# Head by head instead of head pairs on TensorE, and a small two-engine exchange moved to another stage, in a two-block fp32 kernel

## The reference, cut to what matters

```python
    cb = jnp.einsum("bclgn,bcsgn->bcgls", cc, bc)
    y_diag = jnp.einsum("bcgjls,bcsgjp->bclgjp", cb[:, :, :, None] * decay_in, x_)
    y_off = jnp.einsum("bclgn,bcgjpn,bcgjl->bclgjp", cc, prev, jnp.exp(a_cum))
    return (y_diag + y_off).reshape(b, s, h, p)
```

```python
    lb = jax.nn.softmax(lower_bounds.astype(jnp.float32), axis=0)
    lb = jnp.cumsum(lb, axis=0) - lb[0]
    log_f = jnp.logaddexp(jnp.log(jnp.maximum(lb, LB_FLOOR)), jnp.log1p(-lb) + jax.nn.log_sigmoid(z))
```

## Time and profile before

| | |
|---|---|
| median of 3 runs | 1776.52 us (1776.51 to 1776.59) |
| time of the profiled execution | 1776.51 us |
| its span, first to last instruction | 1774.7 us |
| TensorE busy | 1729.7 us, 97% |
| VectorE busy | 1157.8 us, 65% |
| ScalarE busy | 859.0 us, 48% |
| mean DMA rate | 98 GB/s |

### The profile page before, as it was taken

The page is one execution under the profiler, slowest core; times in us unless marked ns, Lnnn a source line. Parts: engine busy times, 40 slices in busy tenths (PEclk is TensorE's granted clock), DMA queues, the critical chain, the costliest instruction groups (busy, mean ns, idle before and its releaser), DMA issues.

```text
span 1774.7 us, 21242 instructions
## 1 busy us (share of the span) xinstructions
PE 1729.7 (97%) x8310; PEld 1421.0 (80%) x8310; DVE 1157.8 (65%) x1699; ACT 859.0 (48%) x1191; POOL 27.0 (2%) x51
## 2 busy tenths in 40 slices
PE   7999999999989999999999999999999999999997
PEld 5788888777768788888888887788888888888886
DVE  6744346777786745677775445767768777768564
ACT  5323234777769423322222333567567567655422
POOL 0000000000000000000000000100000000000000
PEclk9999999999999999999999999999999999999999
DMA  4323222333323222222222332622222222222322
GB/s 154 125 95 120 95 95 89 106 101 98 103 93 103 83 95 95 95 97 102 99 95 95 107 101 102 248 83 73 84 72 72 83 72 72 83 72 83 119 95 83
DMA packets 48419, 174.69 MB, mean 98 GB/s; under 512 B 5552, under 2 KB 5680, under 8 KB 47680
## 3 DMA queue, kind: packets, MB, share of 16 engines
q1 hardware_dynamic: 43712, 155.45, 25.9%
q0 software_dynamic: 4608, 17.89, 3.3%
HBM read 164.87 MB, written 4.26 MB: 95 GB/s over the span
## 4 chain that ended last, share of the span: by engine, by line
PE 83%; DVE 9%; ACT 5%; issue 3%; DMA 0%; DVEq 0%; SPq 0%; ACTq 0%
PE bank L502 73%; PE bank L699 3%; DVE w_low L1330 2%; PE bank L520 2%; ACT w_high L808 2%; ACT L937 1%; DVE seg L1550 1%; DVE Y L1510 1%; PE bank L544 1%; PE bank L708 1%; DVE scaled L1371 0%; PE bank L744 0%; PE bank L733 0%; PE bank L721 0%; DVE Y L1580 0%
## 5 line engine op out<-in xcount | busy, mean ns | idle before, releaser
L502 PE MATMUL bank<-u_high,w_high 128*128 128x512 f32 x1568 | 622.5, 397 | 5.2 <-DVE w_low L1330 5.2
L502 PE MATMUL bank<-u_high,w_low 128*128 128x512 f32 x1568 | 611.1, 390 | 0.0
L502 PE MATMUL bank<-u_low,w_high 128*128 128x512 f32 x1568 | 610.9, 390 | 0.0
L808 ACT ACTIVATE w_high<-raw 128x1024 fp32r<-128x1024 f32 x285 | 300.5, 1055 | 508.9 <-PE bank L502 498.5
L1330 DVE TENSOR_TENSOR w_low<-raw,w_high 128x1024 fp32r<-128x1024 f32 x285 | 348.2, 1222 | 280.4 <-ACT w_high L808 274.9
L502 PEld LDWEIGHTS bank<-u_high,w_high 128*128 128x128 f32 x1568 | 294.5, 188 | 67.6 <-issue 9.5
L502 PEld LDWEIGHTS bank<-u_high,w_low 128*128 128x128 f32 x1568 | 294.4, 188 | 62.5
L502 PEld LDWEIGHTS bank<-u_low,w_high 128*128 128x128 f32 x1568 | 294.7, 188 | 59.7 <-issue 1.7
L1140 ACT ACTIVATE XL<-XL 128x512 f32<-128x512 f32 x56 | 35.3, 630 | 75.2 <-DVE XL L1783 45.8
L1413 DVE TENSOR_TENSOR h_raw<-bank,rs 128x512 f32<-128x512 f32 x44 | 30.4, 691 | 61.8 <-PE bank L502 55.4
L502 PE MATMUL bank<-f_high,w_low 128*128 128x512 f32 x176 | 69.5, 395 | 0.0
(11 more groups left out here) (342 smaller groups left out, 2482.8 us busy)
## 6 DMA issues: line engine op xcount, KB each, us to landing
raw<-stream SPq DMA_DIRECT2D x285, 512.0 KB, 3.2
rows<-running POOLq DMA_DIRECT2D x32, 256.0 KB, 3.9
X<-x_t SPq DMA_DIRECT2D x4, 512.0 KB, 8.4
u_high<-n_high_rows POOLq DMA_DIRECT2D x2, 1024.0 KB, 6.6
u_low<-n_low_rows POOLq DMA_DIRECT2D x2, 1024.0 KB, 9.2
residual<-X POOLq DMA_DIRECT2D x4, 512.0 KB, 7.4
X<-residual POOLq DMA_DIRECT2D x4, 512.0 KB, 6.1
out_t<-X SPq DMA_DIRECT2D x8, 256.0 KB, 2.1
```

The lines of the kernel that those rows point to most:

```text
L502: ins = pe.matmul(acc[:], w[:, k], x[:, at + k], start=start and k == first and j == 0, stop=stop and k == KT - 1 and j == 2)
L808: act.activation(w_high[:, n % HI_RING], raw[:, n % RAW_RING], ACT.Copy).then_inc(hi_done, 1)
```

## The change

Two independent edits. In the first, `heads_y`, which alternated between two heads, becomes `head_y`, which does all matmuls of one head; it is called twice in a row in the same four places, and its wait on `s_mat` asks for one head's operands. In the second, `bounds()` moves on both engines from the `a_out` stage to the `down` stage: on VectorE after the three `ahead` of j = 1, on ScalarE after the three `ahead` of j = 2. A load of the log table ahead of `a_out` goes with it.

```diff
-            def heads_y(g, j):
+            def head_y(g, h):
+                n, j = 8 * g + h, h // 2
+                rows = slice(HEAD_DIM * (h % 2), HEAD_DIM * (h % 2) + HEAD_DIM)
+                hs = slice(h * HEAD_DIM, (h + 1) * HEAD_DIM)
+                if h % 2 == 0:
+                    if j < 2:
+                        pe.wait_ge(st_taken, 2 * g + 2)
+                    else:
+                        pe.wait_ge(s_ytaken, 4 * g + j - 1)
-                pe.wait_ge(s_mat, 16 * g + 4 * j + 4)
+                pe.wait_ge(s_mat, 2 * n + 2)
                 y = side[2 if j % 2 == 0 else 4]
                 for c in range(NCH):
                     cs = slice(c * P, (c + 1) * P)
-                    for state in (False, True)[:2 if c else 1]:
-                        for e in range(2):
...
+                    ins = pe.matmul(y[rows, cs], xdt[:, c, hs], seg[h % 4][:, cs], start=True, stop=c == 0)
+                    if c:
+                        ins = pe.matmul(y[rows, cs], xdec[:, c - 1, hs], cexp[h % 4][:, cs],
+                                        start=False, stop=True)
+                ins.then_inc(s_y, 1)
...
                 if i in (11, 13, 15, 17):
-                    heads_y(g, (i - 11) // 2)
+                    head_y(g, i - 11)
+                    head_y(g, i - 10)
```

```diff
# ScalarE
-            act.preload_act_table_set(LOG_SET)
             for j in range(KT):
                 ahead(("a_out", j))
-                if j == 2:
-                    bounds()
-            table = [LOG_SET]
+            table = [""]
...
             for j in range(KT):
                 for part in range(3):
                     ahead(("down", j, part))
                 if j == 0:
                     act.preload_act_table_set(LOG_SET)
                 else:
+                    if j == 2:
+                        bounds()
                     cast(SECOND_EARLY, j - 1, u_high)
# VectorE
             for j in range(KT):
                 key = ("a_out", j)
                 ahead(key)
-                if j == 1:
-                    bounds()
...
             for j in range(KT):
                 for part in range(3):
                     ahead(("down", j, part))
+                if j == 1:
+                    bounds()
                 residual(2, j, ("down", j, 2), X, both=True, rows=SECOND_EARLY, weight=w_both[:, j:j + 1])
```

More of the change, by code:

```diff
@@ L620, in heads_y @@
                     cs = slice(c * P, (c + 1) * P)
-                    last = []
-                    for state in (False, True)[:2 if c else 1]:
-                        for e in range(2):
[L624 to L633, removed]
+                    ins = pe.matmul(y[rows, cs], xdt[:, c, hs], seg[h % 4][:, cs], start=True, stop=c == 0)
[3 more added lines that the diff above has]
+                ins.then_inc(s_y, 1)
             def group_sum(g):
@@ L1058, in _, with bounds @@
                 act.activation(h1_conv[:], h1_conv[:], ACT.Silu).then_inc(f_silu, 1)
+            def bounds():
+                act.wait_ge(lb_v, 1)
+                act.activation(lbc[:, 1], lbc[:, 1], ACT.Exp).then_inc(lb_a, 1)
+                act.wait_ge(lb_v, 2)
+                act.activation(lbc[:, 1], lbc[:, 1], ACT.Ln).then_inc(lb_a, 1)
+                act.activation(lbc[:, 2], lbc[:, 2], ACT.Ln).then_inc(lb_a, 1)
             for j in range(KT):
@@ L1472, in _ @@
             cp(decay_b[:].rearrange("p c h -> p (c h)"), side[1][:, 0:NCH * HEADS]).then_inc(d_tok, 1)
[L1474 to L1489, removed]
             for j in range(KT):
@@ L1690, in _, with bounds @@
                 dve.wait_ge(f_split, j + 1)
+            def bounds():
+                lbr = par[:, PCOL["lower_bounds_2"]:PCOL["lower_bounds_2"] + 2 * KT]
+                tt(lbc[:, 1], lbr, lbr, ALU.subtract).then_inc(lb_v, 1)
+                dve.wait_ge(lb_a, 1)
+                link(dve.reciprocal(lbc[:, 2], lbc[:, 1]))
+                link(tt(lbc[:, 1], lbc[:, 1], lbc[:, 2], ALU.mult))
+                link(tt(lbc[:, 0], lbc[:, 1], lbc[:, 1], ALU.subtract))
+                link(ts(lbc[:, 5], lbc[:, 0], -1.0, 1.0, ALU.mult, ALU.add))
+                link(cp(lbc[:, 1], lbc[:, 5]))
+                ts(lbc[:, 2], lbc[:, 0], LB_FLOOR, 2.0 ** 40, ALU.max, ALU.mult).then_inc(lb_v, 1)
+                dve.wait_ge(lb_a, 3)
+                link(ts(lbc[:, 2], lbc[:, 2], -40.0 * float(np.log(2.0)), None, ALU.add))
+                link(tt(lbc[:, 3], lbc[:, 2], lbc[:, 1], ALU.subtract))
+                link(tt(lbc[:, 4], lbc[:, 1], lbc[:, 2], ALU.subtract))
             for j in range(KT):
```

## The result

The changed kernel takes 1789.72 us (median of 4 runs, 1789.29 to 1790.95) against 1776.51 us (4 runs, 1776.45 to 1776.59): ratio 1.0076, 95% interval 1.0058 to 1.0093. It is 13.2 us slower; 1792.8 us and a range of 1786 to 1799 us were predicted. The profiled execution took 1789.95 us with a span of 1788.2 us. One execution of the kernel before, beside the first four experiments, took 2167.2 us at a granted clock of 0.75; it is left out of every median and ratio.

What follows compares the result with a forecast made beforehand. TensorE, busy for 97% of the span, was taken to bound the kernel. 1776.5 + 7.3 (head order) + 6.65 (stall) + 2.4 (clock) = 1792.8 us; 8-in-10 range 1786 to 1799 us, the forecast's own 1790 to 1795 us.

Steps and rivals of the forecast that it cites:

- A half of the array keeps 0.109 us a record, two halves run side by side: Head products: each 64-column half was read as taking 0.109 us a record, so head order loses the side-by-side work.
- The growth of a call, 13 x 0.109 = 1.42 us: Each of 16 heads_y calls grows by 1.42 us, only the second head's first record overlapping; 22.7 us in all.
- What reaches the end, 1.6 us from group 0 and 5.7 us from group 3: Scan: waits absorb the additions in groups 1 and 2 and part of group 0's; 7.3 us reaches the end.
- the lower bound of 5.7 us that I gave for part 1: Head order's least cost, group 3 alone; only a half alone at 0.055 us a record would lie below.
- The remainder of group 0: Scan: 5.7 us added in group 0 against waits of 3.8 to 4.3 us leaves 1.4 to 1.9, taken as 1.6 us.
- the separate wait: Scan: waiting separately for the even head was called worth little, since TensorE arrives late there anyway.
- `seg` does not come later because TensorE is later: Scan: ScalarE needs only block n-3, so a TensorE delay of 3 us does not touch its rounding.
- The stall of 6.65 us: Down: TensorE idles before block 8 for rounding and exchange 3.51, residual 0.68, 1.24 to low, low(8) 1.22 us.
- 2.4 us for the clock: Down, behind the stall: 12 matmuls at 0.43 us instead of 0.23 us add 2.4 us, bounds 0 and 2.5.
- The removed table load and the emptied `a_out` stage gain nothing: a_out: VectorE has blocks prepared and ScalarE waits over 4 us per block, so removing exchange and load gains nothing.
- the rival in which the clock holds: Down: no slow matmuls follow the stall, as after the 2.40 us gap; 1790.4 us, chance 0.12.
- the signs that I named: Trace: 0.109 us records, 2.9 us calls, 20 us more scan work, shrunken waits, 6.5 us w_low row, 12 slow matmuls.

Runs made afterwards that it cites:

- the first four experiments: Head order alone, exchange alone moved, VectorE entering the moved exchange one j later, and extra matmuls in the stall; the kernel before took 1776.6 us beside them.
- The run by chunk: Kernel before, with heads_y switching heads after each chunk (2 or 4 records) instead of each product (2 records): 1777.10 us, ratio 1.0002.
- the joint wait: Kernel before with head order and the exchange left in a_out, but both heads waiting for the operands of both: 1782.19 us, ratio 1.0031.
- the run with the filled stall: Changed kernel with heads_y as before, plus 24 unread matmuls on TensorE behind block 7 of down: 1782.85 us, ratio 1.0036.
- e2_bounds_only: Changed kernel with heads_y as before, so only the exchange is moved to down: 1785.48 us, ratio 1.0050 to the kernel before.
- the level exchange: Changed kernel with heads_y as before, VectorE entering the exchange at j = 2 instead of j = 1: 1776.63 us, ratio 1.0000.
- e1_heads_only: Kernel before with head_y and its two calls, bounds() left in a_out: 1781.97 us, ratio 1.0030.
- the last four experiments: Exchange behind the residual, switching heads by chunk, both heads waiting jointly, and head order in groups 0 to 2 only; the kernel before took 1776.5 us beside them.

## Why the prediction held, point by point

- **A half of the array keeps 0.109 us a record, two halves run side by side.** Right; the timeline shows 0.22 us for two records of one head. Their weight loads take longer than that pace, 136 ns each:

```profile
L626 PEld LDWEIGHTS bank<-seg,xdt 128*64 128x64 f32 x256 | 26.8, 136 | 5.6 <-issue 5.6
```

That a weight load between records of one half is not hidden (the rule of the Trainium skill, TensorE: Matmul & The Clock Gate, part 3, "The mechanism", as the prediction read it) is not borne out: at 0.109 us a record, nothing is exposed, although all records use all rows.
- **The growth of a call, 13 x 0.109 = 1.42 us.** This term was too large: 1.14 us. I let one record of the second head run beside the first head; the trace shows the second head starting beside several. The growth is 1.14/0.109 = 10.5 steps and not 13, so three to four of its 14 records are hidden. The run by chunk, with stretches of up to four records at almost no cost (0.05 us a call), agrees.
- **What reaches the end, 1.6 us from group 0 and 5.7 us from group 3.** The mechanism was right and both sizes were off. The scan's cost of 4.7 us even lies below the lower bound of 5.7 us that I gave for part 1, and I had said that only a half alone at 0.055 us a record could bring that; it was the overlap where the heads change. Group 3 cost 4 x 1.14 = 4.6 us. Groups 0 to 2 cost 0.1 us in the changed kernel's trace and nothing measurable when they alone were changed. The remainder of group 0 in the sum, 5.7 - 4.1, hung on the growth: with 4 x 1.14 = 4.6 us added only 0.5 us would be left, and the trace has 0.4. Not even that reached the end: group 1 adds 4.6 us against waits of 5.2 us (five of them, from 418 to 447 us before) and took it up. I had also called the separate wait worth little; with the smaller growth TensorE arrives before the odd head's `seg` at the fourth call, and the trace of the joint wait has two waits there that the separate one avoids.
- **`seg` does not come later because TensorE is later.** Right: 13.7 us of added matmuls in groups 0 to 2 leave the time as it was, which a chain that moves with TensorE would not allow.
- **The stall of 6.65 us.** Right. From the start of ScalarE's rounding at 1001.12 us to VectorE's exit at 1004.63 us it is 3.51 us, the same as in `a_out`; the measured wait is 6.71 us. Moving the residual out took 1.8 us off; entering level with ScalarE took all of it off.
- **2.4 us for the clock.** The mechanism was right: 5.26 us for 12 matmuls, 2.5 us more than at full pace, and the run with the filled stall removes them. That the number fits is luck in part. I took the 12 from the start of one execution; at the start of the other traces here it is 6 to 14 matmuls, which is 1.3 to 2.9 us. The fewest are in `e2_bounds_only`:

```profile
11.65 0.76 PE L520 MATMUL bank<-early_high,w_high 128*128 128x512 f32 x1 [11.65 <-DVE w_low L1329]
...
14.34 0.48 PE L520 MATMUL bank<-early_high,w_high 128*128 128x512 f32 x1
```

Behind the stall it was 12 in all three runs that have slow matmuls there. The Trainium skill's rule on idle gaps between bursts (TensorE: Matmul & The Clock Gate, "HAM oscillation") agrees with both, the slow matmuls behind the idle time and their absence behind the filled one.
- **The removed table load and the emptied `a_out` stage gain nothing.** Nothing contradicts it: the level exchange also does without them there and takes 1776.63 us. No run took the load alone away.

The sum by the measured terms is 4.7 + 6.7 + 2.5 = 13.9 us, less 0.6 us by which this execution was ahead when the scan began, 13.3 us; measured were 13.5 us in the spans and 13.2 us in the medians. The 3 us by which the forecast was high are the growth of a call (4 x 0.28 = 1.1 us) and the remainder of group 0 (1.5 us), and some tenths that start and clock scatter from run to run. The time alone would have misled: 1789.7 us lies nearer to the rival in which the clock holds (1790.4 us) than to the forecast (1792.8 us), and just below the forecast's own range of 1790 to 1795 us. Only the trace tells them apart: the slow matmuls are there (2.5 us), and the scan costs 2.6 us less than forecast.

Of the signs that I named, the pace, the call of about 2.9 us (2.82), the shrunken waits (14.8 to 2.2 us) and the row for `w_low` came. The 20 us of added TensorE time could not show in the window of the scan, which had only 15.0 us free; over the whole execution it rose by 19.5 us, slow matmuls included.

## What to carry to other kernels

A short exchange between two engines can cost a third one the way from the later engine's arrival through the exchange (3.5 us here) and through what stands behind it in the queue of the engine that arrived first (3.1 us here); put both ends at the same place relative to the stream that they serve, and count how many blocks the third engine still has. Matmuls of half width should alternate between the two halves at least every few records: stretches of 4 records cost 0.05 us a call, stretches of 14 cost 1.14 us. Before an added cost is summed up, look at which stretch has waits behind it: here 13.7 us in three groups were free and 4.6 us in the fourth were not.

## What the runs showed of the hardware

- Order between column halves is not strict: with head order, the first L626 records of the second head run among the last L628 records of the first (317.84 to 318.34 us). Stretches of four records alternate at nearly no cost, 0.05 us a call.
- After idle times of 4.88 and 6.71 us in `down` it was the same picture three times, 12 matmuls of 512 columns at 0.43 us each. After the first wait of 11.2 to 12.3 us at the start, the number of such matmuls differed between executions, 6 to 14. After a gap of 2.4 us the clock stayed at 2.4 GHz in the execution of the kernel before, but in the profiled executions of `e1_heads_only` and `e7_joint_wait` a stretch at half clock followed it (0.63 over 4 us in the first) and cost 1.55 us. Such stretches may be part of the scatter of some 2 us between runs: of the 22 runs of the kernel before beside the last four experiments, the four with the lowest mean clock (0.996) took 1777.5 us on average and the other 18 took 1776.4 us. The runs by chunk do not show such an order, and no run here was made to test it.
